# A fused two-block transformer forward pass on one core: in the four moba iterations q, k, v and the turned probabilities are split into high and low parts, and scores and values become three products of parts each

## The reference, cut to what matters

```
proj = rmsnorm(h, g_mix_pre) @ w_in
qa, ka = partial_rope(q heads), partial_rope(k heads)   # the first 32 features turn
s_own = einsum('bhqd,bhkd->bhqk', qc, k_own) * Dh ** -0.5, masked to k_pos <= q_pos
probs = softmax(s_own)
out   = einsum('bhqk,bhkd->bhqd', p_own, v_own)
```

## Time and profile before

| | |
|---|---|
| median of 3 runs | 2799.41 us (2799.23 to 2799.84) |
| the profiled execution's own time | 2799.03 us |
| its span, first to last instruction | 2797.3 us |
| mean granted TensorE clock, share of full | 0.998 |
| PE busy | 2762.0 us, 99% of the span |
| DVE busy | 1782.3 us, 64% |
| ACT busy | 1381.5 us, 49% |
| POOL busy | 36.8 us, 1% |
| the chain that ended last | PE 94%, DVE 3%, ACT 2%, issue 1% |
| DMA, mean | 187 GB/s |
| a 1 MB granule of w_in, issue to landing, median | 5.2 us |

### The profile page before, as it was taken

One profiled execution on the slowest core, in us unless ns is written; L12 is line 12 of the kernel. 1 busy time (PEld: TensorE's weight loads), 2 busy tenths in 40 slices (PEclk: granted clock), 3 DMA queues, 4 the chain that ended last, 5 costly groups with the idle time before them and its releaser, 6 DMA issues.

```text
span 2797.3 us, 39735 instructions
## 1 busy us (share of the span) xinstructions
PE 2762.0 (99%) x14588; PEld 2358.7 (84%) x14588; DVE 1782.3 (64%) x2172; ACT 1381.5 (49%) x1815; POOL 36.8 (1%) x43
## 2 busy tenths in 40 slices
PE   8999999999999999999999999999999999999999
PEld 6888888888888888888877888888888888888887
DVE  7676766665655656556566666665676567657655
ACT  4555554455544434444466555554544344434453
POOL 2000000000000000000000000000000000000000
PEclk9999999999999999999999999999999999999999
DMA  7555546565556556556656555545555555555653
GB/s 265 177 180 166 176 158 197 193 189 182 188 196 194 189 191 190 192 184 197 208 166 207 181 165 180 166 157 185 183 182 195 195 180 182 204 185 182 233 185 136
DMA packets 413226, 521.97 MB, mean 187 GB/s; under 512 B 8544, under 2 KB 320048, under 8 KB 412496
## 3 DMA queue, kind: packets, MB, share of 16 engines
q1 hardware_dynamic: 410384, 510.64, 55.6%
q0 software_dynamic: 2752, 10.11, 1.2%
HBM read 516.51 MB, written 4.21 MB: 186 GB/s over the span
## 4 chain that ended last, share of the span: by engine, by line
PE 94%; DVE 3%; ACT 2%; issue 1%; DMA 0%; SPq 0%; ACTq 0%; DVEq 0%
PE ps L1943 39%; PE ps L1945 19%; PE ps L1953 11%; PE ps L1955 11%; PE ps L1954 11%; PE pw L2061 1%; DVE split L1139 1%; PE pw L2008 0%; DVE X L1252 0%; ACT split L563 0%; PE pw L2062 0%; ACT junk L602 0%; PE pw L2056 0%; PE pw L2050 0%; ACT cross L569 0%
## 5 line engine op out<-in xcount | busy, mean ns | idle before, releaser
L1139 DVE TENSOR_TENSOR split<-raw,split 128x1024 fp32r<-128x1024 f32 x960 | 1156.9, 1224 | 690.9 <-ACT split L563 686.0
L563 ACT ACTIVATE split<-raw 128x1024 fp32r<-128x1024 f32 x960 | 1003.0, 1055 | 812.6 <-PE ps L1955 446.6
L1943 PE MATMUL ps<-X,split 128*128 128x512 f32 x4096 | 1294.4, 397 | 13.4 <-DVE split L1139 9.3
L1945 PEld LDWEIGHTS ps<-X,split 128*128 128x128 f32 x4096 | 770.3, 188 | 182.1
L1945 PE MATMUL ps<-X,split 128*128 128x256 f32 x4096 | 805.7, 278 | 0.0
L1943 PEld LDWEIGHTS ps<-X,split 128*128 128x128 f32 x4096 | 626.6, 189 | 17.1 <-issue 11.0
L1953 PE MATMUL ps<-split,X 128*128 128x512 f32 x1408 | 550.3, 391 | 4.6 <-ACT E L779 1.2
L1955 PE MATMUL ps<-split,X 128*128 128x512 f32 x1408 | 548.1, 389 | 0.0
L1954 PE MATMUL ps<-split,X 128*128 128x512 f32 x1408 | 547.9, 389 | 0.0
L1953 PEld LDWEIGHTS ps<-split,X 128*128 128x128 f32 x1408 | 264.4, 188 | 60.8 <-DVE split L1139 1.9
L1955 PEld LDWEIGHTS ps<-split,X 128*128 128x128 f32 x1408 | 264.3, 188 | 55.1
(11 more groups left out here) (239 smaller groups left out, 1124.2 us busy)
## 6 DMA issues: line engine op xcount, KB each, us to landing
raw<-in_w_up SPq DMA_DIRECT2D x152, 1024.0 KB, 5.5
raw<-in_w_in SPq DMA_DIRECT2D x134, 1024.0 KB, 5.2
raw<-in_w_down SPq DMA_DIRECT2D x108, 1024.0 KB, 5.1
raw<-in_w_out SPq DMA_DIRECT2D x32, 1024.0 KB, 5.1
raw<-in_w_ple_gate SPq DMA_DIRECT2D x32, 1024.0 KB, 5.1
raw<-in_w_br_moba SPq DMA_DIRECT2D x8, 1024.0 KB, 5.5
raw<-in_w_br_diff SPq DMA_DIRECT2D x8, 1024.0 KB, 5.1
raw<-in_w_ple_proj SPq DMA_DIRECT2D x4, 1024.0 KB, 5.1
```

The source lines that it names most:

```text
L563: A(split[:, k % RING, :, 0, :], raw[:, (k // 2) % RING, HALF * (k % 2):HALF * (k % 2) + HALF, :], ACT.Copy).then_inc(hi_done, 1)
L1139: TT(split[:, k % RING, :, 1, :], raw[:, (k // 2) % RING, HALF * (k % 2):HALF * (k % 2) + HALF, :], split[:, k % RING, :, 0, :], ALU.subtr ...
L1943: MM(ps[:, 2 * s + j, :], stay[:, 0, j * P:j * P + P], move, start=start, stop=False, skip_group_check=True)
L1945: ins = MM(ps[:, 2 * s + j, 0:TOK], stay[:, 1, j * P:j * P + P], move[:, 0, :], start=False, stop=stop, skip_group_check=True)
```

## The change

Three sets of work are added and the products are rewritten. After the rotation ACT copies q and k to fp32r (`qk_high`, at its m = 10) and DVE subtracts (`qk_low`, at its m = 10); both go to tiles 8 to 11 of `X2`. v is evacuated without its scaling; ACT makes the scaled high part (`v_high`, first at its m = 12) and DVE the scaled low part (`v_low`, m = 13). In place of `copy_pt`, ACT writes the high part of the turned probabilities (`pt_high`, m = 13), and DVE, at its m = 14 after `lo(14)`, the low part (`pt_low`), which now carries the signal `pt_ready`. PE makes high x high, high x low and low x high for every product of before, in fp32r: `score_split` waits for `qk_split`, `weigh_split` for `v_split` and `pt_ready`. Each head has six products of 128 columns and six of 256 in place of two and two in float32.

```
@@ -217,6 +217,8 @@
     PT = E[:, 9:12, :].rearrange("p a b -> p (a b)").rearrange("p (h s) -> p h s", h=2)
     MX = E[:, 12:16, :]
     qk_sums, qk_norms = small[:, 32:40], small[:, 40:48]
+    QS, VS = X2[:, 8:12], X2[:, 12:14]
+    PS = X2[:, 8:11].rearrange("p k a t -> p (k a t)").rearrange("p (h a t) -> p h a t", h=2, a=2)
 
     x_squares = [E[:, 4 * c:4 * c + 4, :] for c in range(4)]
 
@@ -273,6 +275,7 @@
     h_ready = sem("h_ready")
     x1_hi, x1_ready = sem("x1_hi"), sem("x1_ready")
     rope_done = sem("rope_done")
+    qk_hi, qk_split, v_hi, v_split, pt_hi = (sem(n) for n in ("qk_hi", "qk_split", "v_hi", "v_split", "pt_hi"))
     scores_done, logits_done, exp_done, probs_ready = (sem(n) for n in ("scores_done", "logits_done", "exp_done", "probs_ready"))
     probs_turned, pt_ready, pv_done = sem("probs_turned"), sem("pt_ready"), sem("pv_done")
     o_raw, o_squares, o_sums, o_root, o_normed, o_hi, o_ready = (sem(n) for n in ("o_raw", "o_squares", "o_sums", "o_root", "o_normed", "o_hi", "o_ready"))
@@ -653,6 +656,24 @@
                 act.wait_ge(probs_turned, k + hh + 1)
                 A(PT[:, hh, :], pw[:, hh, 0:384], ACT.Copy).then_inc(pt_ready, 1)
 
+        def qk_high(n):
+
+            act.wait_ge(rope_done, n + 1)
+            A(QS[:, :, 0, :], QK, ACT.Copy).then_inc(qk_hi, 1)
+
+        def v_high(at):
+
+            act.wait_ge(evac_done, at.unit(2) + 1)
+            for key in range(2):
+                ins = A(VS[:, key, 0, :], V[:, key, :], ACT.Copy, scale=norm_col[:, 0, key:key + 1])
+            ins.then_inc(v_hi, 1)
+
+        def pt_high(k, heads):
+
+            for hh in range(heads):
+                act.wait_ge(probs_turned, k + hh + 1)
+                A(PS[:, hh, 0, :], pw[:, hh, 0:384], ACT.Copy).then_inc(pt_hi, 1)
+
         def o_heads(k, tile):
 
             for hh in range(2):
@@ -682,10 +703,13 @@
             def after(m):
                 if isinstance(i, int):
                     set_up_steps(m)
+                if m == 10:
+                    qk_high(i)
                 if m == 12:
+                    v_high(s)
                     softmax_exps(2 * i)
                 if m == 13:
-                    copy_pt(2 * i, 2)
+                    pt_high(2 * i, 2)
                 if m == 15:
                     o_heads(2 * i, 2 * i)
                     gate_a(s, i)
@@ -1165,6 +1189,24 @@
         def evac_values(at, u, k):
             evac_tokens(at, u, k, V)
 
+        def qk_low(n):
+
+            dve.wait_ge(qk_hi, n + 1)
+            TT(QS[:, :, 1, :], QK, QS[:, :, 0, :], ALU.subtract).then_inc(qk_split, 1)
+
+        def v_low(n):
+
+            dve.wait_ge(v_hi, n + 1)
+            for key in range(2):
+                ins = STT(VS[:, key, 1, :], V[:, key, :], norm_col[:, 0, key:key + 1], VS[:, key, 0, :], ALU.mult, ALU.subtract)
+            ins.then_inc(v_split, 1)
+
+        def pt_low(k, heads):
+
+            for hh in range(heads):
+                dve.wait_ge(pt_hi, k + hh + 1)
+                TT(PS[:, hh, 1, :], pw[:, hh, 0:384], PS[:, hh, 0, :], ALU.subtract).then_inc(pt_ready, 1)
+
         def gained_lo(e, c, gain):
 
             for pair in range(2):
@@ -1351,11 +1393,17 @@
                     swap_halves()
                 if m == 9:
                     rope_sum()
+                if m == 10:
+                    qk_low(i)
                 if m == 11:
-                    evac_values(s, 2, 0)
+                    evac(s, 2, V)
                 if m == 12:
                     logits(2 * i, 2 * i, mask_tables, SCALE)
                     normalise(2 * i, 2 * i)
+                if m == 13:
+                    v_low(i)
+                if m == 14:
+                    pt_low(2 * i, 2)
                 if m == 15:
                     evac_normed(s, 3, t[:, (s.u + 3) % 2], mix_rn)
                     o_lo_heads(2 * i, 2 * i)
@@ -1363,7 +1411,7 @@
                     dve.wait_ge(sig_done, i + 1)
             each_half(s, MIX, after)
         moba(0)
-        loop(dve, steps, 4, 12, moba, start=1)
+        loop(dve, steps, 4, 10, moba, start=1)
 
         def diff(i):
             s = At("diff", i, 8, 4)
@@ -2049,6 +2097,24 @@
                 MM(pw[:, 2 + hh, 0:P], QK[:, hh, 0:P], QK[:, 2 + hh, 0:P], start=True, stop=True)
                 MM(pw[:, 2 + hh, P:384], QK[:, hh, P:TOK], QK[:, 2 + hh, :], start=True, stop=True).then_inc(scores_done, 1)
 
+        PRODUCTS = ((0, 0), (0, 1), (1, 0))
+
+        def score_split():
+
+            for hh in range(2):
+                for q, (a0, a1) in enumerate(((0, P), (P, 384))):
+                    for n, (x, y) in enumerate(PRODUCTS):
+                        ins = MM(pw[:, 2 + hh, a0:a1], QS[:, hh, x, q * P:q * P + P], QS[:, 2 + hh, y, 0:a1 - a0], start=n == 0, stop=n == 2)
+                ins.then_inc(scores_done, 1)
+
+        def weigh_split(bank, cs, hh):
+
+            for key, (a0, a1) in enumerate(((0, TOK), (TOK, 384))):
+                for n, (x, y) in enumerate(PRODUCTS):
+                    ins = MM(pw[:, bank, key * P:TOK], VS[:, key, x, cs], PS[:, hh, y, a0:a1],
+                             start=key == 0 and n == 0, stop=key == 1 and n == 2, skip_group_check=True)
+            return ins
+
         def turn_probs(k, heads):
             for hh in range(heads):
                 pe.wait_ge(probs_ready, k + hh + 1)
@@ -2085,15 +2151,18 @@
                 if isinstance(i, int):
                     set_up_steps(m)
                 if m == 12:
-                    pe.wait_ge(rope_done, i + 1)
+                    pe.wait_ge(qk_split, i + 1)
 
                     if not isinstance(i, int):
                         pe.wait_ge(o_ready, 2 * i)
-                    score(2 * i)
+                    score_split()
                 if m == 14:
                     turn_probs(2 * i, 2)
                 if m == 15:
-                    weigh_heads(s, 2, 2 * i)
+                    pe.wait_ge(v_split, i + 1)
+                    for hh in range(2):
+                        pe.wait_ge(pt_ready, 2 * i + hh + 1)
+                        weigh_split(2 + hh, slice(hh * P, hh * P + P), hh).then_inc(pv_done, 1)
             each_half(s, MIX, x1_is(0), before)
         moba(0)
         loop(pe, Chain(None), 4, 0, moba, start=1)
```

## The result

| | before | after |
|---|---|---|
| median of 12 runs | 2799.38 us | 2806.14 us |
| lowest to highest | 2798.55 to 2801.55 | 2804.65 to 2807.94 |
| the profiled execution, its span | 2799.03, 2797.3 | 2805.14, 2803.4 |

The ratio is 1.0024, with a 95% interval of 1.0015 to 1.0032: slower by 6.8 us at the medians, a quarter of a percent. The spans of the two profiled executions differ by 6.1 us; that of after stands 1.0 under its median and that of before 0.4 under its own. When PE reaches the first scores also differs from one profiled execution to the next (56.83 us from the start of the span in after, 57.10 in before, 58.13 in one of the experiments), though nothing on PE ahead of them was changed.

A forecast was written before the change was run, and what follows sets the result against it. PE was taken to bound the kernel, never waiting in the moba iterations. Waits before scores +2.2, before values +3.0 and products +0.5 sum to 5.7, 5.5 with roundings out: 2804.9 us against the median, range 2801.5 to 2811.

The forecast's parts named there:

- the main case: Whole kernel: PE waits before scores and values, narrow products 0.11 us apart; 2804.9 us, good to some 1 us, chance 0.55.
- PE has no slack, ACT and DVE have: Moba iteration: PE busy for all 47.88 us, DVE 32.30, ACT 24.94; added ACT and DVE work costs only if PE waits.
- The wait before the scores: PE waits for qk_high, then qk_low: 0.4 us in iteration 0, 0.6 in three others, +2.2 us in all.
- The wait before the values: PE waits for pt_low, which stands behind hi(14) and lo(14): 0.74 us in each of four iterations, +3.0 us.
- The products: Score and value stages on PE: 1.36 us each, 0.06 more than before; eight stages make +0.5 us.
- The transposes are covered: PE's transposes: normalising ends at 112.1, PE comes at 112.5, so no wait, covered by 0.3 us after the restart.
- The table load behind `v_high`: ACT: v_high, then the 1.28 us table load, before the exponentials, which start 0.6 us late; no load before v_high.
- Rival 1: Narrow products on PE stream at their column rate, 0.058 us: +3.1 us in all, 2802.5 us; chance 0.15.
- rival 2: Narrow fp32r products on PE no faster than float32 ones, 0.22 us: +10.9 us in all, 2810.3 us; chance 0.20.
- Rival 3: v_high switches ACT's tables; second 1.28 us load, PE waits 1.0 us at transposes in three iterations: +8.5, 2807.9 us; chance 0.05.
- Rival 4: Whole kernel gains: every wait hidden and narrow products at column rate, -2.1 us, still within 0.2%; faster given 0.02.

The follow-up runs named there:

- the 256-wide experiment: Changed kernel with the six 128-column score products of an iteration made 256 wide, half of each unused: 2805.77 us, ratio 1.0023 to the kernel before.
- the one arrangement that came out ahead: Changed kernel with q and k split per head, pt_low before lo(14), narrow score squares float32, v_high behind pt_high, v_low behind pt_low: 2799.36 us, ratio 1.0000 to before.

## Why the prediction was right

The forecast was slower, 2804.9 us; measured 2806.14, inside the range of 2801.5 to 2811 and above the 2804 to 2806 of the main case alone. The added time was forecast as 5.5 us; the medians differ by 6.8, the spans by 6.1 and PE's timeline in the moba iterations gives 6.4. The 0.65 between medians and spans lies in how far either profiled execution stands under its own median. The sum itself has a slip: its terms as written, 0.4 + 3 x 0.6, 4 x 0.74 and 8 x 0.056, make 5.6 and not 5.5. The forecast lay on the line of 0.2%, so that the measured difference came out above it is due to terms that were too small, not to anything foreseen. By stage PE's timeline has 2.3 us of waiting before the scores, 3.4 before the values and 0.7 in the products, where the sum had 2.2, 3.0 and 0.5.

- **PE has no slack, ACT and DVE have.** Right. ACT got 7.8 us more busy time and DVE 9.2, and with PE's two waits taken away the kernel was within 0.15 us of before in an iteration.
- **The wait before the scores**, 0.60 predicted in the loop: 0.60 came off when it was removed. `qk_low` ended 0.50 after PE's arrival (106.70 against 106.20), as worked out: 105.47 against 104.98. What PE adds after the wait was 0.12 here too: it starts 0.05 later, and the stage takes 1.48 in place of 1.41.
- **The wait before the values**, 0.74 predicted: 0.85 came off. The chain was right to 0.02 us: `pt_low`, at t + 3.52 against t + 3.5, with 0.55 for the first head (the two cover 1.01). The term too small was what PE adds after a wait. Taken from a diff iteration it was 0.12; here PE starts 118.04 - 117.89 = 0.15 after the subtraction's end, and the stage takes 0.07 more than the 1.37 it takes without a wait, 0.22 together. Why it differs was not tried.
- **The products**, +0.06 per stage: the price of 0.11 for a narrow product was right (0.114), and the 256-wide experiment shows that columns don't set it. That the load does remains argued. The stages took 1.41 and 1.37, not 1.36, so eight cost about 0.7 us, not 0.5. The prediction speaks of halved arithmetic; its own column rate gives less, 1.04 for a stage in place of 1.30. The 0.27 us of one float32 record stands in neither of the groups of rows that it names, but is right: 273 ns at the median of L2049 in the trace of before. The rule that a warm product of 128 columns comes 56 ns after the last (the Trainium skill, TensorE: Matmul & The Clock Gate, back-to-back issue gap) leaves out the load, as that section says itself, and doesn't describe this stream, in which each product has a load of its own: 0.114 here. The same page of the Trainium skill, in its section on LDWEIGHTS, gives a load as its columns divided by 1.2 GHz; an estimate from that is 107 ns for 128 columns, within 7 ns of the 0.114 us.
- **The transposes are covered.** Right in after, but for a wrong reason: the step took them to need both heads' probabilities at once, and so also said that they would be the wait if PE were not held at the scores. With the wait at the scores gone they weren't. Only when PE came another quarter of a microsecond earlier, with the narrow squares in float32 (1.15 us for the stage in place of 1.41), did it pause between the heads.
- **The table load behind `v_high`.** Right: it stands at 109.40, right behind L668, and no second one came; the exponentials start at 110.69, which is 0.6 late against PE's arrival at the scores (110.69 - 106.20 = 4.49; before, 3.90).

Rival 1 (narrow products at their column rate, 0.058) and rival 2 (as dear as float32, 0.22) both fall by the 0.114. Rival 3, a second table load, falls by ACT's timeline, which has none ahead of `v_high`. Rival 4, a gain, falls with rival 1 and by the two waits.

## What to carry to other kernels

Where one engine has no slack, price added work on the others by where it stands in their lists: read the chain from the engine's last handing-over to its next need, with everything that stands in between on each strict queue. Here one line moved up by one step was worth half of the loss. And count products, each with its weight load, not columns: on PE alone, replacing a float32 product by three of fp32r pays at 256 columns (three at 0.117, 0.35, for 1.30 / 2 - 0.22 = 0.43) and loses at 128 (0.34 for 0.22). Even where it pays, the splitting that it needs from ACT and DVE has to be kept out of PE's way: the one arrangement that came out ahead won 0.10 us in 47.88.

## What the runs showed of the hardware

- A wait of PE of 3.1 us was followed by some 6 us at the 1.2 GHz level, and an iteration with it was 2.8 us longer than the wait itself explains; waits of 0.8 us left the granted clock at 1.00.
- fp32r products with a load each came 0.114 us apart at 128 and 0.117 at 256 columns ((1.48 - 0.19) / 11): in this range width is nearly free.
- After a wait for DVE, PE lost 0.12 us in a diff iteration, 0.12 before the scores and 0.22 before the values, beyond the wait itself.
